# Moving the filler work of a cached-block attention loop into two gaps of each step, with one copy for the turned probabilities

## What is computed

```
k_full = cache_k[page_table[:, :c * ppb]].reshape(DB, c, MOBA_BLOCK, H, Dh)
gate = einsum('bthd,bjhd->bhtj', qf, mean(k_full, axis=2))
_, sel = top_k(gate, 3)                      # three of 16 blocks for each query and head
l_sel = einsum('bthd,bhtkd->bhtk', qf, k_g)  # keys and values of the selected blocks
probs = softmax(concatenate([l_sel, l_new]) * scale)
out = probs[sel] @ v_g + probs[new] @ v

# recurrence, for each token t:
S = S * w_t + (S @ a_t) b_t^T + v_t k_t^T ;  y_t = S @ r_t
```

## Time and profile before

| | us |
|---|---|
| median of 3 runs | 1370.97 |
| lowest and highest | 1369.03, 1380.43 |
| the profiled execution, its own time | 1370.97 |
| its span, first to last instruction | 1369.1 |
| PE busy in the span | 1228.4 |
| DVE, POOL, ACT busy | 615.5, 433.3, 416.0 |
| mean granted clock of TensorE | 0.965 |

### The profile page before, as it was taken

One profiled execution on the slowest core, in us unless ns is written; L12 is line 12 of the kernel. 1 busy time (PEld: TensorE's weight loads), 2 busy tenths in 40 slices (PEclk: granted clock), 3 DMA queues, 4 the chain that ended last, 5 costly groups with the idle time before them and its releaser, 6 DMA issues. The chain is left out here.

```text
span 1369.1 us, 33315 instructions
## 1 busy us (share of the span) xinstructions
PE 1228.4 (90%) x14362; PEld 1108.5 (81%) x14362; DVE 615.5 (45%) x1066; ACT 416.0 (30%) x829; POOL 433.3 (32%) x299
## 2 busy tenths in 40 slices
PE   6999997888788888868678999998999999999995
PEld 6998995666566666545368999998999999999994
DVE  6467894443555344543554222324455454440003
ACT  5231322333233322122342222333333333341110
POOL 2343452110110011010023333453655655564430
PEclk9999999999999999998789999999999999999998
DMA  5221218777568678889531222221222222232221
GB/s 224 85 97 62 78 34 339 285 296 270 202 253 309 247 287 343 329 310 362 228 129 62 82 88 93 86 96 62 78 80 91 78 83 88 83 105 80 79 69 69
DMA packets 57252, 216.29 MB, mean 158 GB/s; under 512 B 6609, under 2 KB 6994, under 8 KB 56338
## 3 DMA queue, kind: packets, MB, share of 16 engines
q1 hardware_dynamic: 57106, 214.17, 42.5%
HBM read 207.78 MB, written 6.37 MB: 156 GB/s over the span
## 5 line engine op out<-in xcount | busy, mean ns | idle before, releaser
L642 PE MATMUL ps<-buffer_at 128*128 128x288 f32 (+2 forms) x5760 | 778.7, 298 | 12.2 <-DVE buffer_at L1921 7.2
L642 PEld LDWEIGHTS ps<-buffer_at 128*128 128x128 f32 x5760 | 774.6, 191 | 17.6 <-issue 11.7
L1459 POOL TENSOR_TENSOR buffer_at<-buffer_at 128x1024 fp32r<-128x1024 f32 (+1 forms) x118 | 331.2, 2809 | 387.3 <-ACT buffer_at L1192 386.7
L1192 ACT ACTIVATE buffer_at<-buffer_at 128x1024 fp32r<-128x1024 f32 (+1 forms) x118 | 128.9, 1095 | 289.9 <-PE ps L642 136.1
L1511 POOL TENSOR_TENSOR buffer_at<-buffer_at 128x256 f32<-128x256 f32 x45 | 39.9, 918 | 343.5 <-DVE buffer_at L1751 343.5
L1027 PE MATMUL ps<-buffer_at 128*32 128x128 f32 x2048 | 75.0, 289 | 31.7 <-ACT buffer_at L1313 26.9
L1027 PEld LDWEIGHTS ps<-buffer_at 128*32 128x32 f32 x2048 | 55.7, 114 | 45.4 <-ACT buffer_at L1313 37.7
L1430 ACT ACTIVATE buffer_at<-buffer_at 128x592 f32<-128x592 f32 x44 | 38.8, 883 | 162.5 <-DVE buffer_at L2115 159.3
L2113 DVE TENSOR_TENSOR buffer_at<-ps,buffer_at 128x512 f32<-128x512 f32 x44 | 30.4, 692 | 126.2 <-PE ps L642 126.2
L994 PE MATMUL ps<-buffer_at 128*32 128x256 f32 x1024 | 73.7, 405 | 5.0 <-DMA buffer_at<-in_kvcache 5.0
L1851 DVE TENSOR_REDUCE buffer_at<-ps 128x1 f32<-128x256 f32 (+1 forms) x68 | 27.9, 410 | 100.1 <-PE ps L994 100.0
(11 more groups left out here) (230 smaller groups left out, 1289.6 us busy)
## 6 DMA issues: line engine op xcount, KB each, us to landing
buffer_at<-in_kvcache SPq DMA_DIRECT2D x256, 512.0 KB, 4.9
buffer_at<-in_w_up SPq DMA_DIRECT2D x44, 512.0 KB, 3.5
buffer_at<-in_w_in SPq DMA_DIRECT2D x42, 512.0 KB, 3.5
buffer_at<-in_w_down SPq DMA_DIRECT2D x16, 704.0 KB, 4.0
buffer_at<-in_w_br SPq DMA_DIRECT2D x8, 512.0 KB, 3.5
buffer_at<-in_w_o SPq DMA_DIRECT2D x8, 512.0 KB, 3.5
buffer_at<-in_xin SPq DMA_DIRECT2D x4, 576.0 KB, 6.9
buffer_at<-in_xin SPq DMA_DIRECT2D x1, 2304.0 KB, 11.5
```

Of the source, the lines that this page charges most:

```text
L642: ins = e.matmul(out, lhs, rhs[:, cols], start=(start and i == 0), stop=(stop and i == 2))
L1192: e.activation(hi[:, :, :], raw, ACT.Copy).then_inc(w_hi, 1)
L1459: e.tensor_tensor(lo[:, :, :], raw, hi[:, :, :], ALU.subtract).then_inc(w_lo, 1)
```

## The change

It does six things. The line numbers are those of the kernel before.

1. PE's order in a step becomes: transposes, slot 0, slot 1, values, logits of the next step, slot 2, slot 3. In slots 1 and 3 the unit stage now stands ahead of the chunk stage. ACT and DVE follow the new order, and `gate_step` moves ahead of slot 3 on DVE.
2. `layout()` counts this order and has other costs, another due line, and at most one unit stage for each step passed.
3. The two copies of turned probabilities become one. The buffer gets 32 columns of padding, so that one access pattern of 128 x 256 elements (a stride of 272 between the sequences) reaches the columns of both; no element moves in it.
4. `fill` reads all four page numbers ahead of its wait.
5. The split of the normed input does two lines in each of four steps after the last chunk, where it did one in each of steps 60 to 67.
6. 64 more columns for the padded buffers; later places shift.

What the new plan holds, worked out from the function: two unit stages in step 0, then one in each of steps 1 to 46, all in slot 1; a chunk begins every seven steps (before: six); sample chunk in steps 48 to 56; last chunk in steps 56 to 60, with all four slots filled in 57 to 59; group norm in steps 61 to 65; x lines in steps 61 to 64. Three rows of it, old and new (c is a chunk, its stage behind the point; u a unit's logits, transposes or values):

```diff
@@ weight_of, layout
-        return (7, 7) if k in (4, 6) else (14, 11) if k < 8 else ...
-    return ((7, 7), (14, 11))[k % 2] if k < 14 else ((9, 6), (7, 6), (22, 10))[k - 14]
+        return (7, 7) if k in (4, 6) else (13, 11) if k < 8 else ...
+    return ((7, 7), (13, 11))[k % 2] if k < 14 else ((8, 6), (5, 6), (22, 10))[k - 14]
-            now += ((5, 2)[i % PER == 0], (12, 4)[i % PER == 0], (12, 3)[(i + 1) % PER == 0], 0)[part]
+            now += ((5, 2)[i % PER == 0], 0, (12, 4)[i % PER == 0] + (12, 3)[(i + 1) % PER == 0], 0)[part]
-                if part % 2 and a < 3 * UNITS and ... and unit_free <= now + 5 and 36 * a <= 3 * UNITS * (i + 1):
+                if part % 2 and a < 3 * UNITS and ... and unit_free <= now + 5 and 48 * a <= 3 * UNITS * (i + 1):
-                elif n < STAGES and ... and chunk_free <= now + 5 and now + weight_of(n)[0] / 2 <= 80 + 18.5 * (4 * i + part + 1):
+                elif n < STAGES and ... and chunk_free <= now + (5 if last_unit is None else 8) and now + weight_of(n)[0] / 2 <= 40 + 16.5 * (4 * i + part + 1):
-NORM_STEP = 60
...
@@ the buffers
-        BASE = 44848
+        BASE = 44784
-        pT = [take(4, P) for _ in range(2)]
+        pT_both = [take(2, 272) for _ in range(2)]
+        pT = [t.rearrange("p a b -> p (a b)")[:, 0:4 * P].rearrange("p (a b) -> p a b", a=4) for t in pT_both]
...
@@ SP: fill
+                found = [nc.values_load_multi_w_load_instructions(
+                    ptab[0:1, (2 * p + s) * NPG + 2 * j:(2 * p + s) * NPG + 2 * j + 2], engines=(mybir.EngineType.SP,),
+                    min_val=0, max_val=kvcache.shape[0] - 1)[1] for s in range(2)]
                 if f >= RING:
                     e.wait_ge(sa_pv, fill_step(f - RING) + 1)
                 for s in range(2):
-                    _, pgs = nc.values_load_multi_w_load_instructions(
...
-                    for a, pg in enumerate(pgs):
+                    for a, pg in enumerate(found[s]):
...
@@ PE: the loop
+                attention(UNIT_AT.get((i, 1)))
+                chunk_stage(CHUNK_AT.get((i, 1)))
                 pv_step(i)
-                chunk_stage(CHUNK_AT.get((i, 1)))
-                attention(UNIT_AT.get((i, 1)))
                 if i + 1 < STEPS:
                     qk_step(i + 1)
...
+                attention(UNIT_AT.get((i, 3)))
                 chunk_stage(CHUNK_AT.get((i, 3)))
-                attention(UNIT_AT.get((i, 3)))
@@ ACT: pt_out
-                for s in range(2):
...
-                        d = pT[i % 2][:, 2 * s:2 * s + 2, :].rearrange("p q (a n) -> p (q a) n", a=HP)[:, :, mine]
-                        o = e.activation(d, ps[:, 5, 0:2 * P].rearrange("p (a n) -> p a n", a=2 * HP)[:, :, mine], ACT.Copy)
+                else:
+                    d = pT_both[i % 2][:, :, 0:256].rearrange("p s (q n) -> p s q n", n=32)[:, :, :, 0:16]
+                    o = e.activation(d, ps[:, 5, 0:2 * P].rearrange("p (q s n) -> p s q n", q=2 * HP, s=2), ACT.Copy)
@@ ACT and DVE: end_work
-                if part == 2 and 0 <= i - NORM_STEP < KT:
+                if part == 2 and LAST_CHUNK < i <= LAST_CHUNK + KT // 2:
...
+                    for k in range(2 * (i - LAST_CHUNK) - 2, 2 * (i - LAST_CHUNK)):
...
@@ ACT: the loop
-                o_out(i)
                 chunk_copies(CHUNK_AT.get((i, 1)))
                 attention(UNIT_AT.get((i, 1)))
+                o_out(i)
@@ DVE: the loop
-                att_first(UNIT_AT.get((i - 1, 3)))
+                att_second(UNIT_AT.get((i - 1, 3)))
                 chunk_out(CHUNK_AT.get((i, 0)))
-                att_second(UNIT_AT.get((i - 1, 3)))
                 end_work(i, 0)
+                att_first(UNIT_AT.get((i, 1)))
                 chunk_out(CHUNK_AT.get((i, 1)))
-                att_first(UNIT_AT.get((i, 1)))
...
                 end_work(i, 2)
+                if i + 1 < STEPS:
+                    gate_step(i + 1)
                 if p >= 0 and j == 11:
                     o_rows(p)
+                att_first(UNIT_AT.get((i, 3)))
                 chunk_out(CHUNK_AT.get((i, 3)))
-                if i + 1 < STEPS:
-                    gate_step(i + 1)
```

More of the change, by code:

```diff
@@ L219, in layout @@
         for part in range(4):
-            now += ((5, 2)[i % PER == 0], (12, 4)[i % PER == 0], (12, 3)[(i + 1) % PER == 0], 0)[part]
+            now += ((5, 2)[i % PER == 0], 0, (12, 4)[i % PER == 0] + (12, 3)[(i + 1) % PER == 0], 0)[part]
             for _ in range(1 + part % 2):
                 k = a // 3 % 4 + 1
-                if part % 2 and a < 3 * UNITS and (i, part) not in unit_at and unit_free <= now + 5 and 36 * a <= 3 * UNITS * (i + 1):
+                if part % 2 and a < 3 * UNITS and (i, part) not in unit_at and unit_free <= now + 5 and 48 * a <= 3 * UNITS * (i + 1):
                     if (i, part) in chunk_at:
                         break
-                    work, pause = ((3 * k, 27 + 2 * k), (4 * k, 7 + 2 * k), (3 * k, 7))[a % 3]
+                    work, pause = ((3 * k, 27 + 2 * k), (4 * k, 7 + 2 * k), (2 * k, 7))[a % 3]
                     now = max(now, unit_free) + work
@@ L232, in layout @@
                         last_unit = i
-                elif n < STAGES and (i, part) not in chunk_at and chunk_free <= now + 5 and now + weight_of(n)[0] / 2 <= 80 + 18.5 * (4 * i + part + 1):
+                elif n < STAGES and (i, part) not in chunk_at and chunk_free <= now + (5 if last_unit is None else 8) and now + weight_of(n)[0] / 2 <= 40 + 16.5 * (4 * i + part + 1):
                     if n >= SAMPLE_POS * CHUNK_STAGES + 8 and (last_unit is None or i < last_unit + 4):
@@ L558, in fill @@
                 for s in range(2):
-                    _, pgs = nc.values_load_multi_w_load_instructions(
-                        ptab[0:1, (2 * p + s) * NPG + 2 * j:(2 * p + s) * NPG + 2 * j + 2], engines=(mybir.EngineType.SP,),
-                        min_val=0, max_val=kvcache.shape[0] - 1)
-                    for a, pg in enumerate(pgs):
+                    for a, pg in enumerate(found[s]):
                         e.dma_start(kvring[slot_of(f)][:, 2 * s + a, :],
@@ L1305, in pt_out @@
                     e.wait_ge(sa_pv, i - 1)
-                for s in range(2):
-                    mine = slice(16 * s, 16 * s + 16)
-                    if i % PER == 0:
+                if i % PER == 0:
+                    for s in range(2):
+                        mine = slice(16 * s, 16 * s + 16)
                         d = pT[i % 2][0:NS, 2 * s, :].rearrange("p (a n) -> p a n", a=HP)[:, :, mine]
                         o = e.activation(d, ps[0:NS, 5, 0:P].rearrange("p (a n) -> p a n", a=HP)[:, :, mine], ACT.Copy)
-                    else:
-                        d = pT[i % 2][:, 2 * s:2 * s + 2, :].rearrange("p q (a n) -> p (q a) n", a=HP)[:, :, mine]
-                        o = e.activation(d, ps[:, 5, 0:2 * P].rearrange("p (a n) -> p a n", a=2 * HP)[:, :, mine], ACT.Copy)
+                else:
+                    d = pT_both[i % 2][:, :, 0:256].rearrange("p s (q n) -> p s q n", n=32)[:, :, :, 0:16]
+                    o = e.activation(d, ps[:, 5, 0:2 * P].rearrange("p (q s n) -> p s q n", q=2 * HP, s=2), ACT.Copy)
                 o.then_inc(sa_tc, 1)
@@ L1348, in end_work @@
                     group_norm(GN_AT[i, part])
-                if part == 2 and 0 <= i - NORM_STEP < KT:
-                    k = i - NORM_STEP
+                if part == 2 and LAST_CHUNK < i <= LAST_CHUNK + KT // 2:
                     e.wait_ge(s_x[0], 32)
                     e.wait_ge(st_ready, NCH + 1)
-                    e.activation(xh[:, k, :], x[:, k, :], ACT.Copy, scale=pcol("ln1", k)).then_inc(xh_ready, 1)
+                    for k in range(2 * (i - LAST_CHUNK) - 2, 2 * (i - LAST_CHUNK)):
+                        e.activation(xh[:, k, :], x[:, k, :], ACT.Copy, scale=pcol("ln1", k)).then_inc(xh_ready, 1)
                 if part == 2 and i in (STEPS - 3, STEPS - 2):
@@ L1584, in _ @@
             la.did(e.memset(qbd[:, :, :], 0.0))
-            for t in pT:
+            for t in pT_both:
                 la.did(e.memset(t[:, :, :], 0.0))
@@ L2016, in end_work @@
                     group_norm(GN_AT[i, part])
-                if part == 2 and 0 <= i - NORM_STEP < KT:
-                    k = i - NORM_STEP
-                    e.wait_ge(xh_ready, KT + k + 1)
-                    if k >= 4:
-                        e.wait_ge(gn_mm, HP + 1)
-                    e.scalar_tensor_tensor(out=xlg[:, k, :], in0=x[:, k, :], scalar=pcol("ln1", k), in1=xh[:, k, :],
-                                           op0=ALU.mult, op1=ALU.subtract).then_inc((xs_even, xs_odd)[k % 2], 1)
+                if part == 2 and LAST_CHUNK < i <= LAST_CHUNK + KT // 2:
+                    for k in range(2 * (i - LAST_CHUNK) - 2, 2 * (i - LAST_CHUNK)):
+                        e.wait_ge(xh_ready, KT + k + 1)
+                        if k == 4:
+                            e.wait_ge(gn_mm, HP + 1)
```

(2 more changed lines are left out.)

2 lines of the change are left out of this document (1 added, 1 removed).

## The result

The changed kernel takes 1320.03 us, the median of four runs (1318.17 to 1322.62), where the kernel before took 1370.0 beside it: a ratio of 0.962 with an interval of 0.957 to 0.967, so 50 us faster. Forecast were 1331 and a range of 1312 to 1354. The profiled execution has a span of 1316.7 us, 52.4 less than before's 1369.1.

What follows compares the result with a forecast made beforehand. PE's idle waits for probability copies and the exponential were the main target; 27.2 us (steps 1 to 60), 10.8 (tail) and 1.9 (after the loop), 39.9 off 1369.1, gave 1329.2, forecast 1331, range 1312 to 1354.

Steps and rivals of the forecast that it cites:

- Gap 1: Transposes to values, steps 1 to 60: slots 0 and 1 cover the wait for copies, 23.4 us falling to 3.4.
- Gap 2: Logits to transposes, steps 1 to 60: waits for the exponential and d behind x, 24 us against 17.5 before.
- the dense end: Steps 49 and 57 to 59, x and d in neighbouring slots: d waits for ACT, 7.5 us in all.
- The other waits: Steps 1 to 60: u's copy 0.5 us, summed level 1, gate sum 0, cached blocks 5.0, remaining small waits 7.
- The smaller groups: Smaller PE waits in the loop's steps, taken to keep 7 of 14.5 us.
- the first rival: The blocks' queue limits thirty short steps, 0.6 us lost each, 1344 us; one block needed per 6.3 us; chance 0.17.
- PE's work: Steps 1 to 60: 351.9 us busy, less 4 for the clock (between 0 and 14), giving 347.9.
- The fills: Ring-slot fills get less time, but page numbers are read early: no loss, waits for blocks kept at 5.0 us.
- The tail and after the loop: Steps 61 to 67: 58.7 us against 69.5, 10.8 less; after the loop, earlier x lines, 1.9 less.
- That waits only change place: Loop steps: idle stays at 1.2 us a step, 71.8 in 60 steps, giving 1362 us; chance 0.10.
- The slower clock: Steps 1 to 60 run at granted clock 0.82 because of block waits, 452.5 us, giving 1395; chance 0.05.
- The signs I named: Profile after: L1313 near 4 us, L1286 about unchanged, block waits under 15, L1921 near 5, loop end near 666.

Runs made afterwards that it cites:

- The filled gaps: Kernel before, with two unused 128x128 matmuls between transposes and values in steps with nothing in slot 0: 1364.44 us, ratio 0.995.
- half blocks: Cached blocks after the first three brought in by half, 512 of 1024 columns: changed kernel 1296.67 us, kernel before 1362.26 us.

## Why the prediction was right, and where its sum was wrong

**Gap 1** held. The copies' wait went from 23.4 us to 1.1, forecast 3.4; with the old order it is back at 13.1. The three weight steps cost less than taken.

**Gap 2** was sized as 24 and is less. The 17 steps with an x or u product in slot 2 were to pay 0.53 each, 9.0 us: the view shows 17 waits of 9.2 together, 14 of them of some 0.5. The first steps of a pair cost 0.4 and not 3, and the dense end (x and d side by side) 4.8 and not 7.5. So the sign I expected (24 against 17.5 before, a loss) was wrong: with 9.6 for the exponential and 4.8 for d behind x it is 14.4. The 2.7 for bare steps were to be too short to be listed; all of PE's idle time that no line lists is 1.8.

**The other waits:** the summed level 1.8 (forecast 1), blocks 4.2 (5.0). The idle time of 41.4 against 41 is right in the sum and not in its parts, and that is luck: gap 2 took some 8 to 10 us less than forecast and gap 1 2.3 less, and waits without a releaser grew by 9.4 (15.0 where before had 5.6), which no term had. Two slips of the sum are small beside that. The smaller groups held 13.3 and not 14.5 before, since the 1.2 of the new-key steps stood in gap 1 already; and 388.9 us over 60 steps are 6.5 a step and not the 6.3 of the first rival.

**PE's work** is the term that was mis-sized: 347.9 forecast, 336.3 measured, and with it steps 1 to 60 by 11.2 us. I gave the clock 4 of a possible 14, because I tied it to one wait for a block. The rows give 0.04 x 416.1 - 0.01 x 377.7 = 12.9, to some 4 us either way, as they have two digits. By the trace's records PE had 30.7 us at the half level in this stretch before and 6.8 after; half of the difference, 12.0, is regained. The filled gaps show that covering the gaps at the copy brings part of it by itself. That PE's mean idle share sets the clock is not shown: between 500 and 550 us the kernel before was idle 15.5% at 1.00, and with half blocks 14.5% at 0.96. The remaining 3.6 of the difference fits the closer packing of values and logits (0.89 us apart); that part is argued from the rows, not measured by itself.

**The fills** I took as no loss, and this step failed, though the named wait hardly moved. I had looked only at when a block lands, and the transfers cost time through PE's supply of instructions, which no term had. The two half-block runs put the price that the change added at 13.2 us. The first rival (the blocks' queue takes over) said 13, but by waits for blocks in short steps, and these stayed at 4.2; that the figures agree is luck. Without this price the kernel would have come out at some 1307 us, below the range. The Trainium skill ("DMA: Bandwidth & Descriptors", Specifications) puts the HBM limit of a core at about 358 GB/s. The mean of these 377.65 us is 337, and single slices of the page reach 389, so the limit isn't met as a ceiling here; the price is paid with a mean below it.

**The tail and after the loop.** The five group norm steps take 49.2 (forecast 47), the two bare ones 8.9 (11.7): two misses of opposite sign, 58.15 against 58.7. After the loop the wait fell by 7.16 - 4.9 = 2.3, forecast 1.9. The loop's last step ends at 653.9; 666 was forecast, and the difference is nearly all PE's work.

**Rivals.** That waits only change place is refuted by idle time of 41.4 instead of 71.8. The slower clock is too: it rose. The signs I named came out for L1313 (lower still), the place of x, units and grams, the blocks' waits under 15 and L1921; those for L1286 (about as large as before) and for the end of the loop did not.

**What stays open** is why PE's instruction packets come late beside whole blocks, whether they stand behind the blocks' packets in the DMA engines or wait for memory; no run here tells these apart. Open too is what in the gaps lowers the clock.

## What to carry to other kernels

Before filling a gap look at what each place holds already: here work lay where nothing waited, beside a place where PE waited 0.54 us in step after step, and moving it was worth more than the gap, because PE's clock rose with it. When gaps close, add up the waits without a releaser and the duration of groups that should not have changed, and look whether they come back every so many instructions: transfers that are hardly waited for by name can still cost time, here through the supply of instructions, and halving their bytes measures it. Where a chain runs over other engines, like the group norm's, moving PE's waits about gained nothing here.

## What was not expected of the hardware

- Useless matmuls of 0.61 us in the gaps of 32 steps made the kernel before 0.5% faster (ratio 0.995): mean granted clock 0.98 instead of 0.96 in steps 1 to 58.
- At 337 GB/s of block transfers PE stopped inside groups of matmuls, 1.10 and 1.24 us in one step, with no releaser; at 196 GB/s the same step had no stop and was 2.8 us shorter. Of 19 such stops in 377.65 us, 17 stood at the same place of each 256 instructions of PE, 1.1 to 1.6 us behind the landing of a packet of 16 KB.
- The same PE work in steps 1 to 60 showed 336.3 us busy with whole blocks and 325.3 with half. The clock explains 3.4 of it (6.8 us at the half level against none), and each stop inside a group adds some: 1.44 against 1.05 us for 16 logits.
